# Cache pages laid out by block, and a new order at the end of the mixing stage

## The reference, cut to what matters

```
past_k = cache_k[l][page_table].reshape(n_seq_dec, past_len, ATT_HEADS, HEAD_DIM)
gate = einsum('hqd,hnd->hqn', q, k_mean)          # k_mean: mean of k over each block of 256
_, top = lax.top_k(gate, 3)
s = einsum('hqd,hqskd->hqsk', q, k[selected]) * scale - slope * (qpos - key_pos)
y = softmax(s) @ v[selected]                      # 6 heads of 64
```

## Time and profile before

| | |
|---|---|
| median of 3 runs | 1341.71 us (1341.07 to 1344.0) |
| the profiled execution | 1344.0 us |
| its span, first to last instruction | 1342.3 us |
| instructions | 27940 |
| PE, DVE, ACT, POOL busy | 1317.4, 779.3, 655.0, 245.0 us |
| mean granted PE clock | 0.995 of full speed |
| read and written in HBM | 229.00 and 5.32 MB, 175 GB/s over the span |

### The profile page before, as it was taken

How to read it: one execution, slowest core, us unless ns; L and a number is a source line. 1 busy time by engine, 2 the same in 40 slices (tenths; PEclk the granted TensorE clock), 3 DMA queues, 4 the chain that set the end, 5 groups by cost and what they waited for, 6 DMA issues and landing times.

```text
span 1342.3 us, 27940 instructions
## 1 busy us (share of the span) xinstructions
PE 1317.4 (98%) x10953; PEld 1264.3 (94%) x10953; DVE 779.3 (58%) x794; ACT 655.0 (49%) x733; POOL 245.0 (18%) x373
## 2 busy tenths in 40 slices
PE   6999999999999999999999999999999999999998
PEld 5999999999869999999999999999897799999998
DVE  5555555576666655554555555565856565555544
ACT  4555543435445555543355555334453565555434
POOL 3000000256561000000101000013756220000001
PEclk9999999999999999999999999999999999999998
DMA  6655544657697444444445554446586944444443
GB/s 196 216 164 164 179 141 146 202 177 215 205 318 214 156 139 144 156 149 142 150 157 183 171 180 148 142 148 210 158 257 226 317 136 156 156 142 140 142 159 115
DMA packets 212207, 235.42 MB, mean 175 GB/s; under 512 B 14974, under 2 KB 205192, under 8 KB 212116
## 3 DMA queue, kind: packets, MB, share of 16 engines
q1 hardware_dynamic: 203132, 208.05, 47.7%
q0 software_dynamic: 8864, 26.16, 6.1%
q10 hardware_dynamic: 120, 0.03, 0.0%
HBM read 229.00 MB, written 5.32 MB: 175 GB/s over the span
## 4 chain that ended last, share of the span: by engine, by line
PE 87%; issue 5%; DVE 3%; DMA 2%; SPq 1%; DVEq 1%; POOLq 0%; ACT 0%; POOL 0%; ACTq 0%
PE ps L1309 22%; PE ps L1310 22%; PE ps L1311 22%; PE ps L1396 3%; PE ps L1398 3%; PE ps L1397 3%; PE ps L1543 3%; DMA kbuf<-in_cache_k 2%; SPq L370 1%; PE ps L1580 1%; PE ps L1723 1%; PE ps L1725 1%; PE ps L1724 1%; DVE o_sq L1240 1%; PE ps L1494 1%
## 5 line engine op out<-in xcount | busy, mean ns | idle before, releaser
L649 ACT ACTIVATE w_hi<-w_raw 128x2048 fp32r<-128x2048 f32 x170 | 325.6, 1915 | 539.2 <-PE ps L1311 424.1
L926 DVE TENSOR_TENSOR w_lo<-w_raw,w_hi 128x2048 fp32r<-128x2048 f32 x162 | 371.6, 2294 | 187.4 <-ACT w_hi L649 184.8
L1309 PE MATMUL ps<-h_hi,w_hi 128*128 128x320 f32 x768 | 239.4, 312 | 3.7 <-DVE x L993 2.2
L1311 PE MATMUL ps<-h_hi,w_lo 128*128 128x320 f32 x768 | 238.5, 311 | 0.0
L1310 PE MATMUL ps<-h_lo,w_hi 128*128 128x320 f32 x768 | 238.5, 311 | 0.0
L1309 PE MATMUL ps<-g_hi,w_hi 128*128 128x320 f32 x704 | 218.1, 310 | 0.0
L1311 PE MATMUL ps<-g_hi,w_lo 128*128 128x320 f32 x704 | 217.7, 309 | 0.0
L1310 PE MATMUL ps<-g_lo,w_hi 128*128 128x320 f32 x704 | 217.7, 309 | 0.0
L1310 PE MATMUL ps<-act_lo,w_hi 128*128 128x320 f32 x704 | 216.8, 308 | 0.0
L1311 PE MATMUL ps<-act_hi,w_lo 128*128 128x320 f32 x704 | 216.8, 308 | 0.0
L1309 PE MATMUL ps<-act_hi,w_hi 128*128 128x320 f32 x704 | 216.8, 308 | 0.0
(11 more groups left out here) (284 smaller groups left out, 1787.3 us busy)
## 6 DMA issues: line engine op xcount, KB each, us to landing
w_raw<-in_ffn_w_in SPq DMA_DIRECT2D x90, 1024.0 KB, 5.0
w_raw<-in_ffn_w_out SPq DMA_DIRECT2D x32, 896.0 KB, 4.5
w_raw<-in_w_in SPq DMA_DIRECT2D x22, 1024.0 KB, 5.5
kbuf<-in_cache_k SPq DMA_DIRECT2D x96, 192.0 KB, 3.2
w_raw<-in_ffn_w_out SPq DMA_DIRECT2D x16, 1024.0 KB, 4.8
kbuf<-in_cache_v SPq DMA_DIRECT2D x48, 192.0 KB, 4.9
w_raw<-in_w_out SPq DMA_DIRECT2D x8, 1024.0 KB, 8.2
kbuf<-in_cache_k POOLq DMA_DIRECT2D x32, 192.0 KB, 2.7
```

The costliest lines, as they stand in the source:

```text
L649: act.activation(w_hi[:, slot, :], w_raw[:, slot, :], ACT.Copy).then_inc(hi_done, 1)
L926: dve.tensor_tensor(w_lo[:, slot, :], w_raw[:, slot, :], w_hi[:, slot, :].bitcast(F32), ALU.subtract).then_inc(split_done, 1)
L1309: pe.matmul(out, w_hi[:, slot, w], hi[:, k, :], start=(k == 0), stop=False)
L1311: ins = pe.matmul(out, w_lo[:, slot, w], hi[:, k, :], start=False, stop=(k == k_all - 1))
```

## The change

It has four parts.

1. K pages. The page table is loaded in two halves, so that the even pages of all sequences stand before the odd ones. A half load takes the four even (or odd) pages of a sequence, and page number r of them fills the 32 partitions of row group r, with four pieces of 32 tokens side by side. Bank 2 + r then holds block r, in the order of its tokens. The number of transfers, their bytes and the length of a contiguous piece (1536 B) stay the same.
2. V pages. They come by the same lists, so the even pages fill slots 0 to 3 and the odd ones slots 4 to 7; `smp_out` takes the probabilities in the matching order.
3. `soft_in`. The sum of a block is a plain sum over its bank. The penalty is added by four operations of 256 elements, one for each bank, each of which also gives the maximum of its block; the reduction over 1024 elements at the end is gone.
4. The order at the end of the mixing stage. ACT: `mix_hi(12)`, then `or_high(0)`, `or_high(1)`, then the whole of `exps(3)`, where two of its five parts used to come before `mix_hi(12)`. DVE: after `mix_lo(12)` come `or_lo(0)`, `or_lo(1)`, `soft_sum(3)`, and only then `y_rest(0)` and `or_lo(2)`. PE: after `transpose_probs(3)` comes `transpose_out(1)` with its wait for `y_rest(0)`, and then both tiles of `out_part` in one piece.

```diff
@@ -364,11 +364,11 @@
                 half0 = L * (C_ALL // 2)
                 ffn_in(A["ffn1_w_in"], L, C_F1I, 1)
                 def load_k(p, bb, half):
-                    page = page_numbers(mybir.EngineType.SP, (2 * p + bb) * PAGES + 4 * half, 4)
-                    for j in range(4):
+                    page = page_numbers(mybir.EngineType.SP, 32 * half + (p * 8 + 4 * bb), 4)
+                    for r in range(4):
                         home = k_home(p, bb)
-                        sp_e.dma_start(kbuf[home][:, 4 * half + j, :],
-                                       A["cache_k"][L, page[j]].rearrange("t h d -> t (h d)")).then_inc(k_landed[home][half], 16)
+                        sp_e.dma_start(kbuf[home][32 * r:32 * r + 32, 4 * half:4 * half + 4, :],
+                                       A["cache_k"][L, page[r]].rearrange("(s k) h d -> k s (h d)", s=4)).then_inc(k_landed[home][half], 16)
 
                 ffn_out(A["ffn1_w_out"], L, C_F1O)
                 def mix_load(c):
@@ -391,7 +391,7 @@
 
                 for c in range(3):
                     mix_load(c)
-                sp_e.wait_ge(loaded, 16 * len(C))
+                sp_e.wait_ge(loaded, 16 * (len(C) + 1))
                 wait_apart(sp_e, chunk_used, L * C_ALL + (C_MIX + 2))
                 for half in range(2):
                     load_k(1, 0, half)
@@ -427,7 +427,7 @@
                 def load_v(u):
 
                     for half in range(2):
-                        page = page_numbers(mybir.EngineType.SP, u * PAGES + 4 * half, 4)
+                        page = page_numbers(mybir.EngineType.SP, 32 * half + u * 4, 4)
                         for j in range(4):
                             sp_e.dma_start(v_page(u, 4 * half + j, slice(0, HDIM)),
                                            A["cache_v"][L, page[j]].rearrange("t h d -> t (h d)")).then_inc(v_landed[V_HOME[u]], 16)
@@ -473,7 +473,10 @@
 
         @block.gpsimd
         def _(pool):
-            pool.dma_start(pages[:], A["page_table"].rearrange("(a b) r -> a (b r)", a=1)).then_inc(loaded, 16)
+            for half in range(2):
+                pool.dma_start(pages[:, 32 * half:32 * half + 32],
+                               A["page_table"].rearrange("b (r h) -> h (b r)", h=2)[half:half + 1, :],
+                               allow_slow_non_contiguous=True).then_inc(loaded, 16)
             pool.memset(wbd[:], 0.0).then_inc(prep, 1)
             pool.memset(q_bd[:], 0.0).then_inc(prep, 1)
 
@@ -516,12 +519,13 @@
             with pool.Fori(0, DEPTH) as L:
                 def first_k(bb, half):
 
-                    page = page_numbers(mybir.EngineType.Pool, PAGES * bb + 4 * half, 4)
-                    for j in range(4):
-                        pool.dma_start(kbuf[2 * bb][:, 4 * half + j, :],
-                                       A["cache_k"][L, page[j]].rearrange("t h d -> t (h d)")).then_inc(k_first[bb][half], 16)
-
-                pool.wait_ge(loaded, 16 * len(C))
+                    page = page_numbers(mybir.EngineType.Pool, 32 * half + 4 * bb, 4)
+                    for r in range(4):
+                        pool.dma_start(kbuf[2 * bb][32 * r:32 * r + 32, 4 * half:4 * half + 4, :],
+                                       A["cache_k"][L, page[r]].rearrange("(s k) h d -> k s (h d)", s=4)
+                                       ).then_inc(k_first[bb][half], 16)
+
+                pool.wait_ge(loaded, 16 * (len(C) + 1))
                 wait_apart(pool, stored_st, L * (16 * ST_STORES) + 16)
                 for bb in range(2):
                     for half in range(2):
@@ -608,7 +612,7 @@
                                        cst["own_b"][:].unsqueeze(2).to_broadcast([SMP, NB, HD]), ALU.mult).then_inc(vbd_ok, 1)
 
                 def load_v(u, half):
-                    page = page_numbers(mybir.EngineType.Pool, u * PAGES + 4 * half, 4)
+                    page = page_numbers(mybir.EngineType.Pool, 32 * half + u * 4, 4)
                     for j in range(4):
                         pool.dma_start(v_page(u, 4 * half + j, slice(0, HDIM)),
                                        A["cache_v"][L, page[j]].rearrange("t h d -> t (h d)")).then_inc(v_landed[V_HOME[u]], 16)
@@ -766,15 +770,13 @@
                     act.wait_ge(o_gated, 3 * L + (f + 1))
                     act.activation(o_sq[:, f, :], ps[:, 6, 0:TOK], ACT.Square).then_inc(o_sqd, 1)
 
-                def exps(p, parts=range(5)):
-                    if 0 in parts:
-                        act.wait_ge(sm_bias, L * 4 + p + 1)
-                    for n in parts:
+                def exps(p):
+                    act.wait_ge(sm_bias, L * 4 + p + 1)
+                    for n in range(5):
                         a, b = (256 * n, 256 * n + 256) if n < 4 else (PAST_LEN, PAST_LEN + SMP)
                         ins = act.activation(sp[p][:, a:b], sp[p][:, a:b], ACT.Exp, bias=ss[:, 32 + n:33 + n],
                                              accum_out=ss[:, 40 + n:41 + n])
-                    if 4 in parts:
-                        ins.then_inc(sm_exp, 1)
+                    ins.then_inc(sm_exp, 1)
 
                 def probs_evac(p):
 
@@ -881,13 +883,13 @@
                 root_o(1)
                 probs_evac(2)
                 root_o(2)
-                exps(3, (0, 1))
                 mix_hi(12)
-                exps(3, (2, 3, 4))
+                or_high(0)
+                or_high(1)
+                exps(3)
                 out_evac(1)
                 y_high(0)
-                for f in range(3):
-                    or_high(f)
+                or_high(2)
                 out_evac(2)
                 probs_evac(3)
                 y_high(1)
@@ -1079,15 +1081,14 @@
                     R = slice(0, P)
                     dve.wait_ge(own_done, L * 4 + p + 1)
 
-                    dve.tensor_reduce(ss[:, 0:4], ps[R, 2:6, 0:256].rearrange("p r (c n) -> p c r n", c=4), AXY, ALU.add)
-                    dve.tensor_tensor(sp[p][:, 0:PAST_LEN].rearrange("p (j r n) -> p j r n", j=PAGES, r=4),
-                                      ps[R, 2:6, 0:256].rearrange("p r (j n) -> p j r n", j=PAGES),
-                                      cst["alibi_s"][:].rearrange("p (j r n) -> p j r n", j=PAGES, r=4), ALU.add)
+                    dve.tensor_reduce(ss[:, 0:4], ps[R, 2:6, 0:256], AX, ALU.add)
+                    for c in range(4):
+                        dve.tensor_tensor_reduce(out=sp[p][:, 256 * c:256 * c + 256], in0=ps[R, 2 + c, 0:256],
+                                                 in1=cst["alibi_s"][:, 256 * c:256 * c + 256], scale=1.0, scalar=-3.0e38,
+                                                 op0=ALU.add, op1=ALU.max, accum_out=ss[:, 25 + c:26 + c])
                     dve.tensor_tensor_reduce(out=sp[p][:, PAST_LEN:], in0=ps[R, 5, 256:256 + SMP], in1=cst["alibi_own"][:, p, :],
                                              scale=1.0, scalar=-3.0e38, op0=ALU.add, op1=ALU.max,
                                              accum_out=ss[:, 29:30]).then_inc(sm_in, 1)
-                    dve.drain()
-                    dve.tensor_reduce(ss[:, 25:29], sp[p][:, 0:PAST_LEN].rearrange("p (c n) -> p c n", c=4), AX, ALU.max)
                     dve.drain()
 
                 def soft_bias(p):
@@ -1126,7 +1127,7 @@
                 evac_last(2)
                 dve.drain()
                 dve.tensor_copy(q_smp[:], z[:, ZQA:ZQA + 3, SEQ:]).then_inc(q_own, 1)
-                dve.wait_ge(loaded, 16 * len(C))
+                dve.wait_ge(loaded, 16 * (len(C) + 1))
 
                 es = ext[:, 542:910].rearrange("p (t b n) -> p t b n", t=2, b=NB)
                 dve.wait_ge(pre_tr, L + 1)
@@ -1260,10 +1261,11 @@
                 or_norm(2)
                 dve.drain()
                 mix_lo(12)
+                or_lo(0)
+                or_lo(1)
+                soft_sum(3)
                 y_rest(0)
-                for f in range(3):
-                    or_lo(f)
-                soft_sum(3)
+                or_lo(2)
                 y_rest(1)
                 dve.wait_ge(pt2_done, NB * L + 8)
                 dve.wait_ge(pv_done, (NB // 2) * L + 3)
@@ -1573,8 +1575,9 @@
                     for j in range(PAGES + 1):
                         for g in range(4):
                             rows = P if j < PAGES else SMP
-                            n = 32 if g < 3 or j < 7 else 24
-                            c = 96 * j + 24 * g
+                            at_j = 2 * (j % 4) + j // 4 if j < PAGES else j
+                            n = 32 if g < 3 or at_j < 7 else 24
+                            c = 96 * at_j + 24 * g
                             cols = slice(192 * (g % 2), 192 * (g % 2) + 192)
                             v = v_page(2 * p + g // 2, j, cols) if j < PAGES else v_own[:, cols]
                             ins = pe.matmul(ps[32 * g:32 * g + n, out_bank(p), 0:192], pt_s[p % 2][0:rows, c:c + n], v,
@@ -1731,12 +1734,11 @@
                 smp_out(2)
```

(7 more changed lines are left out.)

## The result

The changed kernel takes 1358.27 us (median of 4 runs, 1357.8 to 1363.18), the kernel before 1342.78 beside it (4 runs). The ratio is 1.0125, 95% interval [1.0098, 1.0151]: 16.8 us slower. The profiled execution took 1359.94 us, its span is 1358.3 against 1342.3, its mean granted clock 0.990 against 0.995. Slower was forecast, from 1340 to 1354.5 us; the time lies above that range.

The account below looks back on a forecast made before the run. PE, busy 98% of the span, was taken as the bound; 1344.0 us profiled plus 2.7 for the layer's end and 4.2 for K pages gave 1350.9, or 1348.6 for the median, with a range of 1340 to 1354.5.

Parts of the forecast that it names:

- soft_in: Softmax input on DVE, 8 times: fused operations save 0.52 us each, 4.2 in all, counted as nothing for PE.
- The 0.14 us at transpose_probs(1): PE's wait for sm_in, which comes 0.7 us later behind the fused operations: 0.14 us may show, once, in layer 0.
- Page table: Two loads at the start instead of one: 0.66 us more of POOL, hidden by PE's 9.5 us wait for x.
- K pages: Loads into 32 partitions move slower, delaying key_scores(2): 0 to 4.5 us per layer, taken as 2.1; +4.2 us in all.
- Tail: End of the mixing stage, twice: transpose_out(1) ahead of out_part ends the stretch 1.35 us later per layer, +2.7 us in all.
- DVE's chain sets it: Layer's end: mix_lo(12), two or_lo, soft_sum(3), y_rest(0) end at 406.81, so PE starts transpose_out(1) at 406.87.
- ACT stays inside this: Layer's end: ACT's exponentials end between 403.3 and 405.6, the last transposes by 406.8, before transpose_out(1) at 406.87.
- Half clock: PE at 1.2 GHz after a stall of 4 us: mentioned only as possible within rival B, with no time added.
- rival B: K loads at 220 GB/s throughout, 4.5 us per layer, 1353.4 us; a 4 us stall might bring the half clock; chance 0.15.
- C: Rival: K loads stay hidden or as fast, only the loss at the layer's end is left, 1344.4 us; chance 0.25.
- D: Rival: nothing shows, an earlier DVE meets the new wait at the layer's end, 1341.7 +- 1.5 us; chance 0.14.
- E: Rival: faster, DVE's 0.52 us reaches PE eight times and two waits at L1723 go, 1335.7 us; chance 0.14.

Follow-up runs that it names:

- a3_soft: Kernel before with only the fused reading of the scores, pages in their old placement: 1341.59 us, ratio 0.9987.
- e1_spread32: Changed kernel with each of SP's K pages written to every fourth of the 128 partitions instead of 32 neighbours: 1353.74 us, ratio 1.0082.
- b1_k64: Changed kernel with each of SP's K pages written to 64 neighbouring partitions, two pieces each, instead of 32: 1362.08 us, ratio 1.0152.
- a4_tail_noact: Kernel before with the new order at the layer's end on DVE and PE, ACT keeping its old one: 1348.78 us, ratio 1.0047.
- c1_fill: Changed kernel with matmuls of constants on PE in the waits for keys and for the last transposes: 1356.83 us, ratio 1.0112.
- g1_tail_fill: Kernel before with the new order at the layer's end, plus matmuls of constants on PE inside the last transposes' wait: 1346.66 us, ratio 1.0020.
- a1_tail: Kernel before with only part 4, the new order at the layer's end on all three engines: 1351.88 us, ratio 1.0056.
- a5_act: Kernel before with only ACT's new order at the layer's end: 1347.82 us, ratio 1.0040.
- a2_pages: Changed kernel without part 4, so with the old order at the layer's end: 1353.92 us, ratio 1.0079.

## Why the prediction was wrong

The sign and both places were right, the size was not: 1350.9 was forecast for the profiled execution, 1359.94 came. Term by term, for one layer:

- **soft_in: right, a little better.** 0.99 us saved instead of 0.52, because the accumulator read lies beside the next operation (0.34 us from one fused operation to the next; I took 0.46). Counted as nothing, since "no wait of PE that the earlier trace rows leaves is released by soft_in"; but the wait for kr_tok, which those rows leave out, is, and falls by 0.7 us in both layers together. It is too small to tell in the time of a3_soft. The 0.14 us at transpose_probs(1) do not show in the waits.
- **Page table: right.** Two loads take 1.18 us on POOL in place of 0.66, and PE waits 9.1 us for x as before.
- **K pages: mis-sized, 2.1 us forecast, 3.24 us measured in layer 0 and 3.40 in layer 1, and 1.26 and 2.18 us of slower matmuls behind.** The failed step is "I take 2.1 us, near the middle, since the rings also carry weights and states at that time". From 330 to 336 us nothing diluted the slow transfers: the rate was 203 to 229 GB/s, just the bound that I had worked out (220). The 4.5 us of that bound did not come in full either. The estimate by the Trainium skill's rule ("SBUF — State Buffer", "Door 1: The DMA port swizzle") was 6.2 us, too much as a wait, but e1_spread32 and b1_k64 agree with the rule of ports that it rests on.
- **Tail: the times were right, what PE waits for and the price were not.** Measured from where PE is ready for the last transposes (408.11 here, 403.25 before, so 4.86 later), I had forecast the exponentials to end at 405.6 + 4.9 = 410.5 if the weights come at 399.36: they ended at 410.46. y_rest(0), forecast at 406.39 + 4.86 = 411.25, began at 411.20; transpose_out(1), 411.73, at 411.93. But "DVE's chain sets it" and "ACT stays inside this" did not hold. The last transposes ended at 411.81 (by 406.8 + 4.86 = 411.66 in the forecast), after y_rest(0) and not before it, and PE waited 2.49 us ahead of them for ACT and not at all ahead of transpose_out(1), where I had put about 1.2. That the two chains end within 0.2 us of each other is why the start came out. DVE's chain is the one that shows only where ACT keeps its old order, in a4_tail_noact. Then I gave the thirty matmuls their time at full clock. The stretch took 6.58 us against the 5.06 forecast (0.46 + 4.6), and 5.05 in a4_tail_noact, c1_fill and g1_tail_fill, where the clock held. That is 1.5 us missing in layer 0 and 1.3 in layer 1 (6.36). a1_tail measured the order at 7.5 us in all, not 2.7.
- **Half clock: the term put at nothing.** It stood only inside rival B, for a stall of 4 us. The prediction's own upper value for the last transposes, 405.6 in place of 403.25, was a stall of 2.35 us, priced as a wait alone. The half clock came behind stalls of 2.5 us, though not always: behind one of the two in a5_act's trace, and behind those in a4_tail_noact's, the clock held. g1_tail_fill shows that the stall brings it: keeping PE busy in the same wait gives back 4.8 of 7.5 us.

For both layers, against the forecast, there are missing: 2.4 us of the wait for keys (3.24 + 3.40 - 4.2), 3.4 of slower matmuls behind it, 0.4 at the start of transpose_out(1) and 2.8 in the stretch behind it (6.58 + 6.36 - 2 x 5.06), together 9.1 of the 9.0 us. That it fits so closely is luck: "issue" is 2.2 us more than before, the wait for kr_tok 0.7 and that for x 0.4 less, and the half clock at 1037 to 1040 us is gone.

Of the rivals, B had the right K rate and the right warning but a price without the clock. C, D and E are refuted: a2_pages shows the keys' part, a1_tail the tail's, and a3_soft that of the 8 us given back to DVE at most 3.6 reach the time.

What stays open: the cause of the "issue" gaps, and what decides whether a wait of 2.5 us is followed by the half clock. Whether a layout exists that gives one block to each bank and still spreads every page over the 128 partitions wasn't tried.

## What to carry to other kernels

When a transfer keeps its bytes but gets another destination, look at which partitions it writes before anything else: here neighbours within one half cost over 40% of the rate, and 32 spread over the whole width kept their keys on time. When PE is the bound, price a new wait as the wait plus the slower matmuls behind it; in the changed kernel that was another 1.3 to 2.2 us for each wait of 2.5 to 3.6 us. Work that stands ahead of a conversion may be what covers its load: before moving it, see when the load lands, not when the conversion began.

## What was not expected of the hardware

- 32 partitions at a distance of four take a page at 371 to 386 GB/s (e1_spread32, 328 to 332 us), like 128; 64 neighbours at 204 to 246 (b1_k64, 329 to 336 us), nearly as slow as 32 (203 to 229).
- Within the 192 short matmuls of key_scores PE stands still for 0.2 to 1.8 us at the same few places (after 174, 166, 150, 116 of them), with nothing in the trace to wait for. The total moves between 1.5 us (kernel before) and 7.5 us (e1_spread32) and is as large as the effects of some edits.
- The half clock can be held off with matmuls of constants, whose result nobody reads: 4.8 us faster in a kernel that stalls 2.5 us twice. It is not tied to stalls alone: the kernel before has it at 1038 us with PE busy.
